# A hybrid GLA / sliding-window / mixture-of-experts block: order of the first loads, place of the experts' transposes, width of silu

## The reference, cut to what matters

```python
u = rms_norm(x)
z = u @ w_in + b_in                      # columns: q_a k_a | v_a | g_a | low rank | q_b | k_b v_b
o_a = gla_chunked(q_a, k_a, v_a, log_a)  # log_a from the low-rank columns, w_a2
o_a = rms_norm(o_a) * gla_norm_w * silu(g_a)
o_b = swa_sink_alibi(q_b, k_b, v_b, sinks)
h = x + concat(o_a, o_b) @ w_out
# hierarchical mixture of experts: 4 groups of 8, top 1 group, top 2 experts in it
for e in range(32):                      # rows that chose e
    y[e] = (silu(xb @ w_gate[e]) * (xb @ w_up[e])) @ w_down[e]
out = rms_norm(h + gated sum of each row's two y)
```

## Time and profile before

| | us |
|---|---|
| median of 3 runs (1945.32 to 1946.11) | 1945.99 |
| the profiled execution | 1948.25 |
| its span | 1946.3 |
| TensorE (PE) matmul busy | 1780.1 (91%) |
| VectorE (DVE) busy | 572.6 (29%) |
| ScalarE (ACT) busy | 498.9 (26%) |
| GpSimd (POOL) busy | 216.1 (11%) |
| mean DMA rate | 195 GB/s |

### The profile page before, as it was taken

How to read it: one execution, slowest core, us unless ns; L and a number is a source line. 1 busy time by engine, 2 the same in 40 slices (tenths; PEclk the granted TensorE clock), 3 DMA queues, 4 the chain that set the end, 5 groups by cost and what they waited for, 6 DMA issues and landing times.

```text
span 1946.3 us, 28769 instructions
## 1 busy us (share of the span) xinstructions
PE 1780.1 (91%) x10562; PEld 1267.3 (65%) x10563; DVE 572.6 (29%) x1111; ACT 498.9 (26%) x1189; POOL 216.1 (11%) x285
## 2 busy tenths in 40 slices
PE   7999999999999999999855999999999999999920
PEld 3566666566665666656634777888878778787710
DVE  1333233333233332433335111111111111111157
ACT  0434332343333342433310111111111111111113
POOL 0000001001011010110002000000000000000045
PEclk9999999999999999999976999999999999999965
DMA  9631133321333312333126789788998899898867
GB/s 322 188 109 61 59 97 108 108 83 36 97 108 108 104 39 73 108 108 108 64 90 235 273 290 325 267 299 308 322 316 296 299 314 329 286 332 303 281 221 319
DMA packets 231525, 379.01 MB, mean 195 GB/s; under 512 B 13715, under 2 KB 118180, under 8 KB 231492
## 3 DMA queue, kind: packets, MB, share of 16 engines
q1 hardware_dynamic: 220548, 340.14, 51.4%
q0 software_dynamic: 10944, 38.41, 5.9%
HBM read 282.04 MB, written 96.47 MB: 194 GB/s over the span
## 4 chain that ended last, share of the span: by engine, by line
PE 39%; DVE 4%; issue 4%; DMA 2%; ACT 1%; POOL 0%; SPq 0%; DVEq 0%; ACTq 0%; POOLq 0%
PE bank L1106 12%; PE bank L1131 12%; PE bank L1095 12%; PE bank L1120 1%; DMA out<-oc 1%; PE bank L1063 1%; DVE hT L1177 1%; DVE oc L1284 1%; DVE column L953 0%; DVE hc L1272 0%; DVE hc L1274 0%; ACT sg L1140 0%; DMA wts<-y_dram,dest 0%; DVE place L953 0%; PE bank L351 0%
## 5 line engine op out<-in xcount | busy, mean ns | idle before, releaser
L283 PE MATMUL bank<-w_in_sb,uT 128*128 128x512 f32 (+1 forms) x1024 | 381.7, 526 | 5.6 <-DMA w_in_sb<-w_in_in 5.6
L283 PEld LDWEIGHTS bank<-w_in_sb,uT 128*128 128x128 f32 x1024 | 177.3, 193 | 175.4 <-issue 168.5
L1095 PEld LDWEIGHTS bank<-xT,wts 128*128 128x128 f32 x2048 | 253.2, 194 | 28.9 <-issue 22.4
L1095 PE MATMUL bank<-xT,wts 128*128 128x128 f32 (+2 forms) x2048 | 258.7, 286 | 8.5 <-issue 6.6
L1106 PE MATMUL bank<-xT,wts 128*128 128x128 f32 (+2 forms) x2048 | 247.9, 282 | 0.0
L1106 PEld LDWEIGHTS bank<-xT,wts 128*128 128x128 f32 x2048 | 245.0, 191 | 0.0
L1131 PE MATMUL bank<-wts,hT 128*128 128x512 f32 x512 | 233.5, 599 | 3.8 <-DVE hT L1177 3.8
L431 PE MATMUL bank<-w_out_sb,mixT 128*128 128x512 f32 x512 | 224.2, 596 | 0.8 <-ACT mixT L508 0.8
L1177 DVE TENSOR_TENSOR hT<-bank,sg 128x256 f32<-128x256 f32 x128 | 54.3, 424 | 444.4 <-PE bank L1106 444.4
L431 PEld LDWEIGHTS bank<-w_out_sb,mixT 128*128 128x128 f32 x512 | 96.6, 191 | 116.9 <-issue 116.9
L1131 PEld LDWEIGHTS bank<-wts,hT 128*128 128x128 f32 x512 | 92.1, 190 | 105.6 <-issue 105.6
(11 more groups left out here) (212 smaller groups left out, 1714.6 us busy)
## 6 DMA issues: line engine op xcount, KB each, us to landing
wts<-w_gate_in SPq DMA_DIRECT2D x32, 2048.0 KB, 9.9
wts<-w_up_in SPq DMA_DIRECT2D x32, 2048.0 KB, 8.9
wts<-w_down_in SPq DMA_DIRECT2D x32, 2048.0 KB, 10.9
y_dram<-nought SPq DMA_DIRECT2D x96, 512.0 KB, 6.0
y_dram<-y SPq DMA_DIRECT2D x32, 512.0 KB, 9.7
x_sb<-x_in SPq DMA_DIRECT2D x17, 512.0 KB, 4.0
w_in_sb<-w_in_in SPq DMA_DIRECT2D x4, 2048.0 KB, 12.8
h_sb<-x_in SPq DMA_DIRECT2D x16, 512.0 KB, 6.3
```

What stands on the lines that cost most here:

```text
L283: m = pe.matmul(bk[name][:, col:col + hi - lo], uT[:, k, :], w_in[:, k, lo:hi], start=k == 0, stop=k == KD - 1)
L1095: m = pe.matmul(G[m_ % 2][:, 0:w], wg[:, k, m_ * P:(m_ + 1) * P], xT[:, k, 0:w], start=k == 0, stop=k == KD - 1)
```

## The change

Three parts. First, `loads` orders SP's queue anew: behind the q_a,k_a columns of w_in only their own bias (semaphore `b_qk_loaded`), then the v columns, then the wait for `xn_ready` and x tile 1, then the g columns, then the other biases and `w_a2` (semaphore `consts`, five loads), then k_b,v_b, low rank and q_b, and last the six other constants (`late_consts`). The waits of the engines follow: VectorE waits for `b_qk_loaded` before q_a,k_a, for `consts` before v, for `late_consts` before it applies `alibi`; TensorE gets a wait for `late_consts` before the product with `cums`, GpSimd's is changed to `late_consts`. These are for tile 0 alone. Second, in `pe_chunk` steps 0 and 1 of the next rows' transposes stand behind the up product, and step 2 between the down halves. Third, in the main loop silu and the product into `hT` work on 160 columns instead of 256.

```diff
@@ -185,19 +185,23 @@
             for dst, src, end in ((S_KB, C_KB, IN_W), (S_LR, C_LR, C_QB), (S_QB, C_QB, C_KB)) if lo == C_LR else ((lo, lo, hi),):
                 sp.dma_start(w_in[:, :, dst:dst + end - src], A["w_in"][0, :, src:end].rearrange("(k p) n -> p k n", p=P))\
                     .then_inc(sem("w_qb_loaded" if src == C_QB else f"w_in_loaded{lo}"), 16)
+            if lo == C_QK:
+                sp.dma_start(b_tm[:, 0:C_V], A["b_in"][0:1, 0:C_V].to_broadcast([P, C_V])).then_inc(sem("b_qk_loaded"), 16)
             if lo == C_V:
-                for dst, src in [(b_tm[:, 0:C_LR], A["b_in"][0:1, 0:C_LR].to_broadcast([P, C_LR])),
+                sp.wait_ge(sem("xn_ready"), 1)
+                sp.dma_start(x[:, :], A["x"][P:2 * P, :]).then_inc(sem("x_loaded"), 16)
+            if lo == C_G:
+                for dst, src in [(b_tm[:, C_V:C_LR], A["b_in"][0:1, C_V:C_LR].to_broadcast([P, C_LR - C_V])),
                                  (b_tm_vb[:, 0:2 * HD], A["b_in"][0:1, C_VB:IN_W].to_broadcast([P, 2 * HD])),
                                  (b_tm_vb[:, 2 * HD:], A["b_in"][0:1, C_LR:C_QB].to_broadcast([P, LOWRANK])),
-                                 (b_fm[:, :], A["b_fm"]), (w_a2[:, :], A["w_a2"]),
-                                 (sinks[:, :], A["swa_sinks"].to_broadcast([P, HB])),
-                                 (gnorm[:, :], A["gla_norm_w"].to_broadcast([P, DV])),
-                                 (cums[:, :, :], A["c_cums"]), (cind[:, :], A["c_cind"]),
-                                 (causal[:, :], A["c_causal"]),
-                                 (alibi[:, :, :], A["c_alibi"])]:
+                                 (b_fm[:, :], A["b_fm"]), (w_a2[:, :], A["w_a2"])]:
                     sp.dma_start(dst, src).then_inc(sem("consts"), 16)
-                sp.wait_ge(sem("xn_ready"), 1)
-                sp.dma_start(x[:, :], A["x"][P:2 * P, :]).then_inc(sem("x_loaded"), 16)
+        for dst, src in [(sinks[:, :], A["swa_sinks"].to_broadcast([P, HB])),
+                         (gnorm[:, :], A["gla_norm_w"].to_broadcast([P, DV])),
+                         (cums[:, :, :], A["c_cums"]), (cind[:, :], A["c_cind"]),
+                         (causal[:, :], A["c_causal"]),
+                         (alibi[:, :, :], A["c_alibi"])]:
+            sp.dma_start(dst, src).then_inc(sem("late_consts"), 16)
         sp.dma_start(w_out[:, 0:HA, :], A["w_out"][0, 0:VA, :].rearrange("(k p) n -> p k n", p=P)).then_inc(sem("w_out_loaded"), 16)
         for gg in range(2):
             rows = A["w_out"][0, VA + gg * 4 * HD:VA + (gg + 1) * 4 * HD, :]
@@ -218,7 +222,7 @@
                 dst = blocks[b] if isinstance(b, int) else blocks[bass.ds(b, 1)].rearrange("o p r c -> (o p) r c")
                 sp.dma_start(dst, src).then_inc(sem("y_cleared"), 16)
 
-    FIRST, CONSTS, W_OUT = 5 * 16, 11 * 16, 7 * 16
+    FIRST, CONSTS, LATE, W_OUT = 5 * 16, 5 * 16, 6 * 16, 7 * 16
 
     rider = (sem("first_consts"), FIRST)
 
@@ -443,6 +447,8 @@
 
         if on("bb"):
             wait(pe, sem("ls_ready"), i + 1)
+            if isinstance(i, int) and i == 0:
+                wait(pe, sem("late_consts"), LATE)
             for n in range(2):
                 m = pe.matmul(bk["bb"][:, n * QKA:(n + 1) * QKA], cums[:, n, :], ls[:, :], start=True, stop=True)
             m.then_inc(sem("bb_done"), 1)
@@ -602,7 +608,7 @@
                     .then_inc(sem("p_ready"), 1)
         if new:
             if isinstance(i, int) and i == 0:
-                wait(v_, sem("consts"), CONSTS)
+                wait(v_, sem("b_qk_loaded"), 16)
             if not isinstance(i, int) or i >= 1:
                 wait(v_, sem("s_done"), 4 * i)
                 dve.tensor_copy(kb[:, :, 0:CHUNK], kb[:, :, P:WK])
@@ -638,6 +644,8 @@
             m.then_inc(sem("S_ready"), 1)
         if new:
             wait(v_, sem("v_done"), i + 1)
+            if isinstance(i, int) and i == 0:
+                wait(v_, sem("consts"), CONSTS)
             dve.tensor_tensor(v[:, par, :], BK["v"][:, :], b_tm[:, C_V:C_G], ALU.add).then_inc(sem("v_ready"), 1)
             if not isinstance(i, int) or i + 1 < NT:
                 normalise_x(i + 1)
@@ -689,6 +697,8 @@
             dve.scalar_tensor_tensor(g_t[:, :], g[:, :], 0.0, g_t[:, :], ALU.min, ALU.subtract).then_inc(sem("lsg_ready"), 1)
 
             wait(v_, sem("pTc1_done"), i)
+            if isinstance(i, int) and i == 0:
+                wait(v_, sem("late_consts"), LATE)
             for n in range(4):
                 wait(v_, sem("s_done"), 4 * i + n + 1)
                 heads = slice(4 * (n // 2) + n % 2, 4 * (n // 2) + 4, 2)
@@ -738,7 +748,7 @@
                  (sem("v2_ready"), i - 1))
         if new:
             if isinstance(i, int) and i == 0:
-                wait(po, sem("consts"), CONSTS)
+                wait(po, sem("late_consts"), LATE)
             wait(po, sem("mixA_ready"), i)
             wait(po, sem("sig_ready"), i + 1)
             pool.tensor_tensor(gm[:, :], g[:, :], g_t[:, :], ALU.mult).then_inc(sem("gm_step"), 1)
@@ -1111,7 +1121,7 @@
 
         pe_gate(pe, pre, n, w)
         pe_up(pe, pre, n, w)
-        next_x((0,))
+        next_x((0, 1))
         wait(pe, sem(f"{pre}w_down_loaded"), 16 * (n + 1))
         after(pe, pre, "h_ready", 4 * n + 4)
         if P < w <= MAIN:
@@ -1131,13 +1141,14 @@
                 m = pe.matmul(YB[half][:, :], hT[:, k, 0:P], wd[:, k, half * 512:(half + 1) * 512], start=k == 0, stop=k == KF - 1)
             m.then_inc(sem(pre + "d_done"), 2 if w == P and half == 0 else 1)
             if half == 0:
-                next_x((1, 2))
+                next_x((2,))
 
     def act_chunk(act, pre, n):
+        n_ = MAIN if pre == "m_" else CAP
         for m_ in range(KF):
             after(act, pre, "g_done", 4 * n + m_ + 1)
             after(act, pre, "h_ready", 4 * (n - 1) + m_ + 1)
-            act.activation(sg[:, m_, :], G[m_ % 2][:, 0:CAP], ACT.Silu).then_inc(sem(pre + "sg_ready"), 1)
+            act.activation(sg[:, m_, 0:n_], G[m_ % 2][:, 0:n_], ACT.Silu).then_inc(sem(pre + "sg_ready"), 1)
         wait(act, sem(f"{pre}y_stored"), 80 * (n + 1))
         for part in (1, 0):
             after(act, pre, "d_done", 3 * n + 2 - part)
@@ -1170,11 +1181,12 @@
                 .then_inc(sem(pre + "xT_ready"), 1)
 
     def dve_h(v_, pre, n):
+        n_ = MAIN if pre == "m_" else CAP
         for m_ in range(KF):
             after(v_, pre, "sg_ready", 4 * n + m_ + 1)
             after(v_, pre, "u_done", 4 * n + m_ + 1)
             after(v_, pre, "d_done", 3 * n)
-            nc.vector.tensor_tensor(hT[:, m_, :], U[m_ % 2][:, 0:CAP], sg[:, m_, :], ALU.mult)\
+            nc.vector.tensor_tensor(hT[:, m_, 0:n_], U[m_ % 2][:, 0:n_], sg[:, m_, 0:n_], ALU.mult)\
                 .then_inc(sem(pre + "h_ready"), 1)
 
     def dve_y(v_, pre, n, part):
```

## The result

The changed kernel takes **1926.07 us**, median of 4 runs (1924.96 to 1928.28), against 1946.05 of the kernel before (4 runs, 1945.32 to 1949.06): a ratio of 0.9896, 95% interval 0.9879 to 0.9913, so 20.0 us off, where 20.4 were forecast. Its profiled execution took 1924.96 with a span of 1923.0, that is 23.3 less than the profiled execution before.

What follows compares the result with a forecast made beforehand. TensorE was taken as the bound, never short of work nearly everywhere; 6.45 (start) + 12.5 (transposes) + 1.4 (silu) = 20.4 us off 1945.99 gives 1925.6 us, range 1920 to 1931.

Steps and rivals of the forecast that it cites:

- The forecast's mechanisms: TensorE: no load wait from 29 to 45, no hT wait in experts, clock 1.00 up to 60; forecast chance 0.80.
- The start's 6.45 us: TensorE's 3.43 wait for w_in's g columns and the g projection's slow clock behind it go: 6.45 us.
- The transposes' 12.5: Moved transposes cover TensorE's hT wait before the down products: 18 x 0.47 + 14 x 0.29 = 12.5 us.
- a bound: If the first instruction of a down half costs 0.1 more after transposes than counted, 3 us less gain.
- the wait is covered even without the narrower VectorE step: Experts: last hT product is ready 0.82 after transposes start; eight last 0.88, covering it without the 160-column product.
- Silu's 1.4: In narrow experts TensorE's wait for the first silu shrinks: 18 x 0.08 = 1.4; wide ones counted nothing, up to 1.1.
- such pauses as a surprise: Other surprises, such as changed code placing, with TensorE's loop pausing when a width comes up first: chance 0.02.
- Both ways of counting: Landing of start loads by bytes or from today's: g 26.2 or 27.6, low rank 31.1 or 32.9, q_b 37.0 or 38.3.
- the engines would be kept busy across the early wait for the scaled x: DMA engines stay busy until 12.1 with q,k columns, then bias and v columns, so SP's early wait costs nothing.
- The thinnest cover, q_b's: q_b columns land 1.2 to 2.5 before TensorE wants them at 39.5; rival, wait moves there: 1930.4, chance 0.08.
- it could only come earlier: Third x tile, issued at 67.6, lands at 74.2, earlier if it moves; ScalarE squares it at 76.7.
- Clock falls by transposes: Rival: eight transposes drop TensorE's clock in down products, 3.0 us a fall, 2022 with one per expert; chance 0.02.

Runs made afterwards that it cites:

- late_before_qb: The changed kernel with the six late constants (1029 KB) put ahead of the q_b columns of w_in again: 1927.89 us, ratio 0.992.
- before: The kernel before the change, nothing altered: 1946.05 us, median of 4 runs.
- silu_only: The kernel before with only silu and the product into hT going from 256 to 160 columns: 4.9 us faster (interval 2.7 to 7.0).
- before_look2: The second of two further profiled executions of the kernel before, nothing changed: 1946.36 us.
- warm: The changed kernel with five unused matmuls of 128 columns ahead of the q,k projection of tile 0: 1924.77 us, ratio 0.99.
- both: The changed kernel with a one-column silu at the top of each expert (early table load) and the five early unused matmuls: 1920.07 us, ratio 0.9874.

## Why the prediction was right, and where not

- **The forecast's mechanisms happened.** No transfer releases TensorE between 29 and 45, no `hT` does in the experts, the clock is 1.00 from 28 to 64. The transposes of the next x stand at 46.95 (47.6 forecast), the q_b projection at 38.87 (39.5), up to down at 7.95 (8.0), the silu wait at 0.17 and silu at 0.303, as forecast.
- **The start's 6.45 us was mis-sized: 2.9 measured.** The step that failed is the one that took 3.43 of waiting and 9.90 - 6.88 of slow clock from a single execution and subtracted them from a median. It is right for that execution (7.1 came off it); in four others with the same order the wait was 1.22 to 2.31 and the fall of the clock, 3.02, did not occur.
- **The transposes' 12.5 measured 11.6 by the trace.** Narrow experts gave 0.48 for 0.47. Wide ones gave 0.21 for 0.29, because the tail product, free of any wait now, still starts 0.97 behind the first of eight transposes (1220.67 and 1221.64 in the timeline) and not 0.88: the place where an instruction behind transposes starts later than I counted, which the prediction had as a bound. The statement that the wait is covered even without the narrower VectorE step is right but for 0.04 per narrow expert.
- **Silu's 1.4 measured 2.2.** The term left out the nine experts of 144 rows, in which the wait shrank by the same 0.08; it was named as a bound (up to 1.1 in wide experts) and belonged into the sum. In the five of 160 rows it was nothing.
- **So the 20.0 is luck in part.** The terms as measured, 11.6 and 2.2 by spacing and 2.9 for the start, make 16.7, against 20.2 (interval 16.9 to 23.5). The other 3.5 are the shorter pauses ahead of the gate products of the first nine experts and the clock that no longer falls behind one of them: 9.4 us in the mean of six traces, 5.9 in three. The prediction put them at nothing (it names such pauses as a surprise, with a chance of 0.02). The start was priced 3.5 too high and this left out, and the two errors happened to be of about the same size.
- **Cover at the start.** Both ways of counting held: g landed at 9.9 + 16.3 = 26.2, by bytes exactly; low rank at 31.8 (31.1 to 32.9 forecast), q_b at 37.2 (37.0 to 38.3). That the engines would be kept busy across the early wait for the scaled x was wrong: from 12 to 13 us they moved 143 GB/s where they had 389 before. It cost g nothing, since from 13 to 20 they moved 398 where they had 350. The thinnest cover, q_b's, was 1.7, and `late_before_qb` shows what is behind it: a wait of 0.95 and no fall of the clock, in the one trace there is.
- **The third x tile moved the other way.** I wrote that it could only come earlier. It was issued at 69.9 instead of 67.6, after SP's clears of y, which began 1.5 later (59.27 and 57.76), and landed at 76.3. ScalarE waited 1.13 us. TensorE, as forecast for a miss, did not.
- **Clock falls by transposes:** none, not with eight and not with sixteen. On the contrary, the falls that the expert loop has with the old place, one or two in each of six traces, are gone in the seven with the new one. The mixer's transposes, on which the prediction based this, were the right rows to read.

## What to carry to other kernels

Before a wait is priced at the length that one profiled execution shows, look at a second one: a transfer that is late by 2 us can carry a fall of the clock that four of five executions don't pay. A wait on a producer is best covered by work of the same engine that is due soon anyway, and then a faster producer is worth less than it was alone (by the spacings silu is worth 5.4 us alone and 2.9 in company). Once the wait is gone, look at what the producer does first when it gets its input: here a table load, worth about 5 us. And before a sum is called right, compare several traces of either kernel in the places that were priced at nothing: here they held 3.5 us.

## What the runs showed of the hardware that was not expected

- The granted clock behind an idle stretch of TensorE does not go by its length alone. At the g projection it was 1.00 behind 1.22, 1.51, 2.30 and 2.31 us and 0.50 behind 3.43 and 7.06. In the expert loop it stayed at 1.00 behind 2.51 (`before`, second expert) and 2.92 (`silu_only`, seventh), and fell to 0.50 behind 2.17 and 2.42 (`before_look2`, ninth and second) and 2.58 (`before`, seventh). Behind the wait of 2.93 or 2.94 for `qdkiT`, which ends between 61 and 74 us, every trace shows it down to between 0.50 and 0.53 for a time, before and after the change.
- A fall costs 3.0 us in 16 products of 512 columns at the start, and 1.3 to 1.7 in a gate product of 64 instructions.
- The first instructions of the q,k projection are slow although the clock row says 1.00 from 12 us on: the run of 32 takes 15.60 to 16.80 us in the old order where 32 x 0.43 = 13.8 would do, the run of 48 takes 22.63 to 23.80 in the new where 20.6 would. Ten rows of small products in the 2.2 us before it bring it to 20.87 (`warm`) and 21.60 (`both`). The loss, 1.7 to 3.0 us without the modelled end, differs between executions, and with it the length of the wait behind it.
- The same loads in the same order had g's columns in place at 30.2 to 30.8 us in four executions and at 32.3 in a fifth.
- The second, third, seventh and in some traces the ninth expert cost up to 4.5 us more than the others between the down load and the next gate load, with TensorE idle for "issue" in front of its gate product. The second is the second of 128 rows, the third the first of 160, the seventh the second of 160 and the ninth the second of 144, so a width's first use does not explain them.
